# A scan's first chunk loaded inside the projection ahead of it, and the output projection begun inside the scan

## What is computed

```
layer 0:  h = rms(x) * g;  proj = h @ w_in            (gates z, o; features xBC, q, k; values v)
          y_a = SSD scan over chunks (state per head) ; y_b = mLSTM scan over chunks (memory per head)
          x = x + concat(rms-normed y_a * silu(z), rms-normed y_b * silu(z)) @ w_out      (2048 -> 1024)
layer 1:  h = rms(x) * g;  q, k, v, z = h @ c_w_in
          differential attention with linear position bias, rms-norm, silu(z) gate;  x = x + y @ c_w_out
out = rms(x) * final_g
```

## Time and profile before

| | us |
|---|---|
| median of the runs | 1629.3 |
| the profiled run | 1628.29 |
| its profiled span | 1626.6 |
| PE busy | 1546.7 (95%) |
| DVE, ACT, POOL busy | 899.4, 649.4, 584.1 |

### The profile page before, as it was taken

The page is one execution under the profiler, slowest core; times in us unless marked ns, Lnnn a source line. Parts: engine busy times, 40 slices in busy tenths (PEclk is TensorE's granted clock), DMA queues, the critical chain, the costliest instruction groups (busy, mean ns, idle before and its releaser), DMA issues.

```text
span 1626.6 us, 23740 instructions
## 1 busy us (share of the span) xinstructions
PE 1546.7 (95%) x9153; PEld 1328.2 (82%) x9153; DVE 899.4 (55%) x1466; ACT 649.4 (40%) x1272; POOL 584.1 (36%) x333
## 2 busy tenths in 40 slices
PE   6899999999999979999699999999999999999797
PEld 5688989898999967778588877888888888877686
DVE  5766878584944338888445434345545234563633
ACT  5443434352532214434243433335554433555421
POOL 4335444444444326565454531124122113221110
PEclk9999999999999979999799999999999999999899
DMA  4124232333333254566385531013112102103622
GB/s 159 52 73 135 86 122 95 113 115 93 117 104 104 72 188 162 165 197 199 123 282 193 171 104 53 26 34 97 53 33 65 33 14 69 68 28 123 237 74 104
DMA packets 149756, 176.36 MB, mean 108 GB/s; under 512 B 8590, under 2 KB 125458, under 8 KB 148626
## 3 DMA queue, kind: packets, MB, share of 16 engines
q1 hardware_dynamic: 149650, 174.91, 32.7%
HBM read 122.46 MB, written 52.43 MB: 108 GB/s over the span
## 4 chain that ended last, share of the span: by engine, by line
PE 46%; DVE 2%; ACT 1%; DMA 1%; issue 1%; POOL 1%; SPq 0%; POOLq 0%; ACTq 0%; DVEq 0%
PE a_ps L2195 21%; PE a_ps L2240 4%; PE a_ps L2215 3%; PE a_ps L2146 3%; PE a_ps L2147 3%; PE a_ps L2148 3%; PE a_ps L2227 2%; PE a_ps L2307 2%; PE a_ps L2308 2%; PE a_ps L2309 2%; PE a_ps L2248 1%; POOL a_w_lo L1713 0%; PE a_ps L2163 0%; DMA a_q_lo<-z 0%; DMA z<-b_y_T 0%
## 5 line engine op out<-in xcount | busy, mean ns | idle before, releaser
L1713 POOL TENSOR_TENSOR a_w_lo<-b_w_raw,a_w_hi 128x1024 fp32r<-128x1024 f32 x72 | 172.5, 2397 | 376.1 <-DVE a_w_hi L1973 253.6
L352 POOL TENSOR_TENSOR p_w_lo<-b_y_T,p_w_hi 128x1024 fp32r<-128x1024 f32 x60 | 156.2, 2605 | 212.9 <-ACT p_w_hi L411 212.9
L2195 PE MATMUL a_ps<-a_h_hi,a_w_hi 128*128 128x512 f32 x384 | 160.8, 419 | 2.9 <-DVE a_h_lo L1951 2.9
L2195 PE MATMUL a_ps<-a_h_hi,a_w_lo 128*128 128x512 f32 x384 | 151.2, 394 | 0.0
L2195 PE MATMUL a_ps<-a_h_lo,a_w_hi 128*128 128x512 f32 x384 | 150.5, 392 | 0.0
L841 PE MATMUL p_bank<-p_w_hi,p_hi_s 128*128 128x256 f32 x512 | 145.0, 283 | 0.0
L841 PE MATMUL p_bank<-p_w_lo,p_hi_s 128*128 128x256 f32 x512 | 144.9, 283 | 0.0
L841 PE MATMUL p_bank<-p_w_hi,p_lo_s 128*128 128x256 f32 x512 | 144.9, 283 | 0.0
L645 DVE SCALAR_TENSOR_TENSOR b_w_raw<-p_out_raw,p_cols,b_w_raw 128x1024 f32<-128x1024 f32 x60 | 119.8, 2004 | 13.7 <-ACT b_w_raw L442 12.3
L841 PE MATMUL p_bank<-p_w_hi,p_hi 128*128 128x256 f32 x384 | 108.9, 283 | 0.0
L841 PE MATMUL p_bank<-p_w_lo,p_hi 128*128 128x256 f32 x384 | 108.7, 283 | 0.0
(11 more groups left out here) (378 smaller groups left out, 3933.7 us busy)
## 6 DMA issues: line engine op xcount, KB each, us to landing
b_y_T<-in_ab_w_in SPq DMA_DIRECT2D x33, 512.0 KB, 4.4
tok<-p_out_raw SPq DMA_DIRECT2D x64, 256.0 KB, 2.5
b_w_raw<-in_ab_w_out SPq DMA_DIRECT2D x32, 512.0 KB, 3.8
b_w_raw<-in_c_w_in SPq DMA_DIRECT2D x32, 512.0 KB, 4.1
c_gz<-tok SPq DMA_DIRECT2D x8, 1536.0 KB, 10.4
feat<-b_w_raw SPq DMA_DIRECT2D x20, 512.0 KB, 3.4
c_fe<-feat SPq DMA_DIRECT2D x8, 1280.0 KB, 6.8
yt<-b_y_T SPq DMA_DIRECT2D x8, 1024.0 KB, 10.9
```

Of the source, the lines that this page charges most:

```text
L352: gp.tensor_tensor(w_lo[s % SLOTS][:, :, :], operand(n, split_of(n, p))[:, :, :], w_hi[s % SLOTS][:, :, :].bitcast(F32), ALU.subtract).the ...
L1713: gp.tensor_tensor(w_lo[:, w, :], w_raw[u % W_RAW][:, :], w_hi[:, w, :].bitcast(F32), ALU.subtract).then_inc(S["l_wlo"], 1)
L2195: mm = pe.matmul(o, x, y, start=(k == 0 and q == 0), stop=(k == KT - 1 and q == 2))
```

## The change

1. The block of the projection no longer waits at its end for the stores of tokens. SP loads chunk 0 while the projection's last two blocks are still being multiplied: features in n = 11, the first gate, the keys, gains and skip vector in n = 12, the two other gates after the store of quarter (1, 1). They go to `w_raw`, `y_raw` and `y_T`, which are free by then. The values of chunk 0, whose stores are the last, are loaded in the scan, behind the wait for the stores. POOL waits for those before it clears `cmem`, which now lies where the stores read from.
2. In chunk 0 PE transposes the features before the first decays and no longer waits for the gains and the masks first.
3. `w_hi`, `w_lo` and the first six `y_hi`, `y_lo` live outside the three stages, as PSUM does. In the projection the same memory holds its weight slots and three of its left operands; in the scan, slots 2 to 4 of `w_hi` hold the gates of the even chunks from 2 on.
4. In the scan SP loads the raw tiles and pieces of units 0 to 7, ACT and DVE and POOL make the halves of units 0 to 5, and PE runs all 24 matmuls of units 0 to 3: tiles 2, 3 and 1 of units 0 and 1 behind chunk 7's state update, those of unit 2 between the two halves of chunk 7's turn, those of unit 3 after it, and tile 0 of all four at the end (banks 0 and 1 serve the turns). POOL makes `w_lo` of units 0 and 1 in chunk 7 right behind the state's decay, so ahead of the skip sum, that of unit 2 behind the gate, 3 to 5 at the end.
5. The middle in layer 2 begins with unit 4. Its gains are loaded straight into columns (a load of single elements) instead of as rows that PE transposes. The rows of x are loaded four units later than before.
6. Two of the three clearings of semaphores between scan and layer 2 are gone.

The diff, cut to what the prediction speaks of:

```diff
+MID_EARLY = 4
...
+                if n == nb - 2:
+                    for s in (0, 1):
+                        sp.wait_ge(S[f"c_stored{s}"], 16 * 2 * nf)
+                    load_first["features"](sp)
+                if n == nb - 1:
+                    sp.wait_ge(S["l_wlo"], seq(n, "7") + 1)
+                    for r in (0, 2):
+                        sp.wait_ge(S[f"t_stored{r}"], 16 * (nt - 2))
+                    load_first["gate_a"](sp)
+                    sp.wait_ge(S["l_wlo"], seq(n, "5") + 1)
+                    load_first["keys"](sp)
...
-            for s in (0, 1):
-                sp.wait_ge(S[f"c_stored{s}"], 16 * 2 * nf)
-            for r in range(8):
-                sp.wait_ge(S[f"t_stored{r}"], 16 * nt)
+                        if n == nb - 1 and (i, k) == (1, 1):
+                            sp.wait_ge(S["l_wlo"], STEPS)
+                            load_first["gates_b"](sp)
...
-            load_consts(sp)
-            for n in (0, 1):
-                load_chunk(sp, chunk, feat, tok, n, n)
+            for r in ahead["t_stored"]:
+                sp.wait_ge(r, 16 * TOK_BLOCKS)
+            load_values(sp, chunk, tok, 0, 0)
+            load_chunk(sp, chunk, feat, tok, 1, 1)
             over(sp, 0, TILES - 2, body)
-            store_y(TILES - 3, 1)
-            for u in range(W_RAW):
-                load_ahead_w(sp, ahead, w_mid, u)
             for i in (0, 1):
                 sp.wait_ge(S[f"y_out{i}"], 16 * 2)
-            for i in (0, 1):
-                load_ahead_y(sp, ahead, yt, i)
+            for u in range(W_RAW):
+                load_ahead_y(sp, ahead, yt, u)
+                load_ahead_w(sp, ahead, w_mid, u)
+            store_y(TILES - 3, 1)
             store_y(TILES - 2, 0)
-            store_y(TILES - 1, 1)
+            for u in range(W_RAW, UNITS_RING + W_RAW):
+                sp.wait_ge(S["l_wlo"], u - W_RAW + 1)
+                load_ahead_w(sp, ahead, w_mid, u)
+                sp.wait_ge(S["d_ylo"], u - 1)
+                load_ahead_y(sp, ahead, yt, u)
+                if u == UNITS_RING - 1:
+                    store_y(TILES - 1, 1)
...
+                if behind_first(n):
+                    pe.wait_ge(S["sel_ok"], n + 1)
+                    pe.wait_ge(S["d_cmem"], n * 4)
+                    decays(n, par, 0)
+                    decays(n, par, 1)
+                    features()
+                else:
+                    features()
+                    pe.wait_ge(S["masks_ok"], 4)
+                    pe.wait_ge(S["sel_ok"], 1)
+                    decays(n, par, 0)
+                    decays(n, par, 1)
+                    pe.wait_ge(S["cols_ok"], 1)
+                    pe.wait_ge(S["drow_ok"], 1)
+                    pe.wait_ge(chunk["keys_landed"], 16)
...
+            def mid_products(u, tiles):
+                pe.wait_ge(S["l_wlo"], u + 1)
+                pe.wait_ge(S["d_ylo"], u + 1)
+                for t in tiles:
+                    for j in (0, 1):
+                        c, out = slice(j * BLK, (j + 1) * BLK), ps[:, 2 * t + j, :]
+                        if u == 0 and t == 1:
+                            pe.wait_ge(S["d_state"], 2 * TILES)
+                        pe.matmul(out, y_hi(u)[:, t * P:(t + 1) * P], w_hi[:, slot(u), c], start=(u == 0), stop=False)
+                        pe.matmul(out, y_hi(u)[:, t * P:(t + 1) * P], w_lo[:, slot(u), c], start=False, stop=False)
+                        mm = pe.matmul(out, y_lo(u)[:, t * P:(t + 1) * P], w_hi[:, slot(u), c], start=False, stop=False)
+                return mm
+
             over(pe, 0, TILES - 1, body)
             outputs(TILES - 1, 1, (TILES - 1) // 2)
+
+            pe.wait_ge(S["d_cmem"], 4 * TILES)
+            for u in (0, 1):
+                mid_products(u, (2, 3, 1))
             pe.wait_ge(S["d_y"], 2 * TILES)
             turn(TILES - 1, 0)
+            mid_products(2, (2, 3, 1))
             turn(TILES - 1, 1)
+            mid_products(3, (2, 3, 1))
+            pe.wait_ge(S["d_yT"], 4 * TILES)
+            for u in range(MID_EARLY):
+                mid_products(u, (0,)).then_inc(S["p_w"], 1)
...
+                if isinstance(n, int) and n == TILES - 2:
+                    high_y(0)
...
+            act.wait_ge(S["d_yb"], TILES - 1)
+            high_unit(0)
+            high_y(1)
+            high_unit(1)
             memory_squares(TILES - 1)
+            high_y(2)
+            high_unit(2)
             ssd_squares(TILES - 1)
             ssd_norm(TILES - 1)
+            for u in range(3, UNITS_RING):
+                high_y(u)
+                high_unit(u)
...
+            for r in ahead["t_stored"]:
+                gp.wait_ge(r, 16 * TOK_BLOCKS)
             gp.memset(cmem[:, :, :], 0.0).then_inc(S["zero_ok"], 1)
...
+                spare(0)
+                spare(1)
...
+                spare(2)
...
-            over(gp, 0, TILES, body)
+            over(gp, 0, TILES - 1, body)
+            body(TILES - 1, 1, (TILES - 1) // 2, low_unit)
+            for u in range(3, UNITS_RING):
+                low_unit(u)
...
+                    if isinstance(n, int) and n == TILES - 2 and k == 0:
+                        low_y(0)
...
+                if isinstance(n, int) and n == TILES - 1:
+                    low_y(1)
...
+            low_y(2)
             ssd_means(TILES - 1)
             turn(TILES - 1, 0, 1, (TILES - 1) // 2)
+            low_y(3)
             turn(TILES - 1, 1, 1)
+            for u in range(4, UNITS_RING):
+                low_y(u)
...
-            with nc.allow_non_contiguous_dma(reason="a column of 128 gains"):
-                sp.dma_start(row_in[0:KT, :], norm_g).then_inc(S["rows_in"], 16)
+            with nc.allow_non_contiguous_dma(reason="columns of 128 gains"):
+                sp.dma_start(cols[:, :], norm_g.rearrange("k p -> p k")).then_inc(S["cols_in"], 16)
                 sp.dma_start(g_col[:, :], subln_g.rearrange("a p -> p a")).then_inc(S["const_in"], 16)
             for i, r in enumerate(lams):
                 sp.dma_start(lam_in[:, i, :], r.broadcast_to([P, F])).then_inc(S["const_in"], 16)
-            for u in range(2, MID + W_RAW):
+            for i in (0, 1):
+                sp.wait_ge(ahead["y_out"][i], 16 * TILES // 2)
+            for u in range(UNITS_RING + W_RAW, MID + W_RAW):
                 if u < MID:
                     load_y(u)
                 load_unit(u)
-                if u == 4:
-                    for i in (0, 1):
-                        sp.wait_ge(ahead["y_out"][i], 16 * TILES // 2)
-                if 4 <= u < 8:
-                    load_row(u - 4)
-                if 10 <= u < 14:
-                    load_row(u - 6)
+                if 8 <= u < 12:
+                    load_row(u - 8)
+                if 12 <= u < 16:
+                    load_row(u - 8)
...
-            low_unit(0)
-            low_unit(1)
+            low_unit(UNITS_RING)
...
-            for u in range(2, MID + 2):
+            for u in range(UNITS_RING + 1, MID + 2):
...
-            for u in range(MID):
+            for u in range(UNITS_RING, MID):
...
-            dve.wait_ge(S["rows_T"], 1)
-            dve.tensor_copy(cols[:, :], ps[:, 7, 0:KT]).then_inc(S["cols_ok"], 1)
-            dve.wait_ge(S["cols_ok"], 1)
-            for i in range(4):
+            for i in range(UNITS_RING, UNITS_RING + 2):
...
+            dve.wait_ge(S["cols_in"], 16)
...
-            pe.wait_ge(S["rows_in"], 16)
-            pe.wait_ge(S["pool_ok"], 3)
-            pe.transpose(ps[:, 7, 0:KT], row_in[0:KT, :], ident[0:KT, 0:KT]).then_inc(S["rows_T"], 1)
-            pe.wait_ge(S["w_high"], 1)
-            pe.wait_ge(S["a_yhi"], 1)
-            for bank in range(8):
-                if bank == 7:
-                    pe.wait_ge(S["cols_ok"], 1)
-                pe.matmul(ps[:, bank, :], y_hi(0)[:, bank // 2 * P:(bank // 2 + 1) * P],
-                          w_hi[:, slot(0), bank % 2 * BLK:(bank % 2 + 1) * BLK], start=True, stop=False)
-            for u in range(MID - LATE):
+            for u in range(MID_EARLY, MID - LATE):
...
+        chunk = dict(first_fe=w_raw[:, :, :].rearrange("p a (f t) -> p (a f) t", t=P),
+                     first_keys=y_raw[:, 0, :].rearrange("p (f t) -> p f t", t=P),
+                     first_gz=[y_T[0][:, 0:D], y_T[1][:, 0:D], y_T[1][:, D:2 * D]],
+                     row_in=y_raw[0:AB_OUT_T, 1, 0:P], drow=y_raw[0:1, 1, P:P + SSD_HEADS],
...
+        def load_features(sp):
+            sp.dma_start(chunk["first_fe"], feat0[0:KEYS, :, 0:P].rearrange("f p t -> p f t")).then_inc(chunk["fe_landed"][0], 16)
+
+        def load_keys(sp):
+            sp.dma_start(chunk["first_keys"], feat0[KEYS:FEAT_T, :, 0:P].rearrange("f p t -> p f t")
+                         ).then_inc(chunk["keys_landed"], 16)
+            sp.dma_start(chunk["drow"], ab_d_skip).then_inc(chunk["const_in"], 16)
+            half_rows = AB_OUT_T // 2
+            for i, g in enumerate((ab_ssd_norm_g, ab_ml_norm_g)):
```

(8 more changed lines are left out.)

205 lines of the change are left out of this document (112 added, 93 removed).

## The result

| | before | after |
|---|---|---|
| median | 1629.09 (6 runs, 1623.95 to 1629.96) | 1616.69 (6 runs, 1610.0 to 1619.74) |
| profiled run | 1628.29 | 1616.27 |
| span | 1626.6 | 1614.5 |

The account below looks back on a forecast made before the run. PE, busy 95% of the span, was taken as the bound, so only its work or standing counts. 1628.29 − 7.2 (seam 1) − 15.8 (seam 2) = 1605.3 profiled, plus 1.0 for the median: 1606, range 1601 to 1615.

Parts of the forecast that it names:

- nothing in chunks 1 to 6 moves: Scan after chunk 0's outputs: its period was to stay as before.
- the projection at nothing: Projection: keeps its instruction lists, so no change in time beyond gaps against the clock of 1 to 2 us.
- the clock of the head: Scan's start: PE's clock falls as before at about 578.6, so only the features gain, 1.3 to 1.4 us.
- Seam 1, 7.2: Between projection and scan: earlier block start and loads bring chunk 0's outputs to 592.7 to 592.8, gain 7.2 us.
- the low end of the bounds: Seam between projection and scan: all remaining PE pieces at low clock, outputs at 594.1, gain 5.9 us.
- Rival A: Seam between projection and scan: clock stays full, 4.7 us more gain, 1601.6; chance 0.12.
- Rival B: Scan's tail: not fed, loads landing late leave ACT late twice, 6.8 us lost, 1613; chance 0.12.
- rival E: Projection's 574 us: operands in shared memory collide with store or cast traffic; at 5%, 28.7 us lost, 1635; chance 0.07.
- signs of being wrong: PE waiting over 2 us before unit 2 or 3, different head clock, or projection's end moved over 1 us from 574.3.
- Seam 2, 15.8: Between scan and middle: units 0 to 3 multiplied in the scan's tail, middle starts with 28 units left, gain 15.8 us.
- Column loads: Start of layer 2: gains loaded as 1024 single elements cost 0, within bounds of 0 to about 13 us.
- The step from profiled run to median: Final sum: median taken as 1.0 us above the profiled run, 1605.3 to 1606.3.

Follow-up runs that it names:

- second series: The changed kernel unaltered, timed once more beside the kernel before: median 1613.76 us (ratio 0.9901).
- the halves later: Changed kernel with both halves of unit 0's piece of yt made in chunk 7 instead of chunk 6: 1610.41 us.
- equal placement: Changed kernel with two small tensors allocated before the shared memory, so shared slots and private operands share a remainder by 4096 bytes: 1606.58, 1606.75, 1609.37 us.
- low half 0 ahead: Kernel of padding and loads ahead, with POOL making unit 0's low half ahead of the state's decay: 1611.59 us.
- all three behind the gate: Kernel of padding and loads ahead, with all three early low halves made behind the gate: 1613.73 us.
- both repairs: Changed kernel with equal placement and the first output-projection loads issued ahead of chunk 7's: 1608.98 us.
- padding: 28 unused floats per partition: ahead of the projection's own operands in the changed kernel, 1610.92 us; between left operands and weight slots in the kernel before, 1629.58.
- loads ahead: Changed kernel with padding, and the first loads for the output projection issued ahead of chunk 7's own loads: 1609.77 us.
- low half 1 behind the power: Kernel with both repairs, with POOL's low half of unit 1 behind skip sum and first norm's power: 1605.62 us.

## Why the prediction was wrong

It missed by 10.7 us (1616.69 for 1606), and 1.7 beyond the range. The second series, 1613.76, lies inside the range, so whether the median lies in it depends on which group the runs fell in; the forecast itself is missed by both, and no run of the changed kernel was below 1610.0. Three steps failed: "nothing in chunks 1 to 6 moves" (4.2 us), the projection at nothing (4.1, of which 2.6 to 2.9 by placement), and the clock of the head (1.3). Against the profiled run the sum was 1605.3 and 1616.3 came out.

- **Seam 1, 7.2: right in size (7.8), wrong in its clock.** The block came as early as worked out: PE stood from 578.4 to 580.7, 2.3 us for the 6.5 of before. But the step "the clock falls as before at about 578.6" failed, and its reading was off: a share of 0.60 in the microsecond from 578, between the levels 1 and 0.5, puts the fall of before at 578.2, after 3.9 us without work and not 4.3. In the changed kernel the features and the first decays ran at full clock, the fall came about 8 us behind the projection's end and lasted 13.7 us, into chunk 0. With chunk 0 the seam's gain is 5.9; that it equals the low end of the bounds, and that the head's 7.8 is near 7.2, is luck. Head and chunk 0 took 48.3 before, and 42.4 in three profiles (the changed kernel twice, the halves later). They took 40.9 to 41.4 in four others of the same head code (equal placement, low half 0 ahead, all three behind the gate, both repairs) and 39.4 in three (padding, loads ahead, low half 1 behind the power), where the clock was low for 3.4 us twice. The kernel before took 44.5 with padding, its head unchanged and low for 10.2 us in place of 20.5: that much of the 48.3 could go without any change of the seam. Rival A (no fall) was not seen in any profile.
- **"Nothing in chunks 1 to 6 moves": failed, 4.2 us.** The excerpt of the diff shows one cast and one subtraction put in chunk 6, and the sum has no term for them. Their size is nothing (0.69), but they wait for a load, and I looked at the load's queue only in the scan's tail, not behind chunk 7's own three loads (the features alone are 1280 KB). What stood in DVE's list behind the waiting instruction was on PE's path. Rival B named the mechanism (loads not in time), with its place wrong: before unit 2 PE didn't wait, before the turn 0.98 and before unit 3 0.59. Both repairs tried, the halves one chunk later and the loads one chunk earlier, took the 27.4 back to 23.2 and 23.7.
- **The projection: rival E's place, at 4.1 us and not at 28.** It was held at 0.07 with a price of 5%; it came as 0.7%, of which 2.6 to 2.9 us by placement, and not by traffic, as it supposed. The text had "at other addresses only" as the reason against it, and the addresses were the cause. No row of before gives its size, so it could only have been a term of unknown size above nothing, with the range wider on that side. The prediction's own signs of being wrong named a move of the projection's end by more than 1 us and another clock in the head; both came.
- **Seam 2, 15.8: right (14.5).** The state update, the 96 matmuls and the start of layer 2 came at the worked-out distances, 29.35 for 28.1. The 1.3 missing are the waits at the turn and before unit 3 (1.6 for the 1.0 allowed) and 0.7 in the matmuls and turns; the block change took the 1.5 it was given. The slack of 2 us at the turn was used up, since I moved DVE's memory norm by POOL's 2.4 and kept its length. In the timeline after, POOL and DVE:

```profile
781.51 2.38 POOL L1378 TENSOR_TENSOR s_y<-s_y,c_gz 128x1024 f32<-128x1024 f32 x1
783.86 2.59 POOL L1343 TENSOR_TENSOR b_w<-b_w_raw,b_w 128x1024 fp32r<-128x1024 f32 x1
781.57 5.96 DVE L1525 SCALAR_TENSOR_TENSOR s_y<-s_y,s_rms,c_gz 128x256 f32<-128x256 f32 x4 [0.91 <-POOL s_rms L1372]
```

The norm met gate and low half 2, took 5.96 for the 3.17 of the earlier trace rows, and ended at 787.5. The rule of the Trainium skill was cited for that ("SBUF — State Buffer", "Who interferes with whom") with one or two waits of up to 2.4; the traces agree with it in the instructions on two operands, and the 13.4 to 15.8 that the prediction gave for two waits holds the measured 14.5. The instruction that took 1.71 us above reads one tensor, so it lies outside the part of the rule that was cited. How much of the 5.96 is waiting for POOL is not shown by itself.
- **Column loads: right.** The 1024 elements were issued in 0.38 us, not 9, below even the 1.12 taken from 128 elements; their landing is not in the trace. PE waited for nothing behind them, and the rest of the kernel has its old length, 808.9 for 808.8.
- **The step from profiled run to median.** 1.0 above the profiled run was a reading of one run; the changed kernel's own runs lie 9.7 us apart.

## What to carry to other kernels

An instruction that is added to an engine's list costs its wait, not its duration: follow each of its inputs back to the load, and look at what stands ahead of that load in its queue, chunk by chunk. When a buffer is moved, compare the addresses of the two operands of each matmul before and after, not only the memory's size, and look at the distance of starts: PE's busy time was 400 of 400 us in both from 100 to 500. Before a difference of some 3 us is given to a change, compare two profiles of the same code, stretch by stretch, with the time at the low clock beside each: here the first 105 us alone differed by 1.9. A fall of the clock behind a short stop can give back part of a wait that is removed there, as in seam 1; take head and following chunk together.

## What the runs showed of the hardware

Operand placement: with both operands of a 512-column matmul at equal remainders by 4096 bytes, starts were 0.227 apart; at other remainders 0.232 to 0.234. The remainders follow from the sizes in the order of allocation, counted from the first tensor: 1168 and 1280 bytes gave 0.2324, 1280 and 0 gave 0.233, 1168 and 0 gave 0.234, and 0 and 0 or 1168 and 1168 gave 0.227. With 256 columns equal remainders gave 0.120 and the others 0.1183 to 0.1199, so unequal placement was sometimes faster there.

DVE and POOL: DVE instructions of four elements per partition took 1.71 and 2.27 us in place of 0.16 while POOL subtracted two 128 x 1024 operands, and ended when it did.

SP's queue: one issue took 8.83 us behind three large loads and a store, against 0.43 for the next, and ended when the last of these loads landed. One chunk earlier in the list, behind loads that had landed, the same issue took 0.33.

Clock: behind stops of PE of 2.3 us the granted clock fell at once (padding, 576.9) or 8 us after the projection's end (the changed kernel, 586.6), and was low for 3.4 to 13.7 us.
